# A transformer block on one Trainium2 core: keys, values and two retention heads join the projections that run while the conditioning weights load

## What is computed

```python
c_act = silu(c)
mod = c_act @ w_ada + b_ada                    # sh1, sc1, gt1, sh2, sc2, gt2
h = rms_norm(x, g_mix) * (1 + sc1) + sh1
rq, rk, rv, rg, aq, ak, av = split(h @ w_in + b_in)
ret = retention(rq, rk, rv, rg)                # 4 heads of 256, pairs rotated
att = window_sink_attention(aq, ak, av, sinks) # 16 query heads, 2 key heads of 64
x = x + gt1 * (concat(ret, att) @ w_out)
h = rms_norm(x, g_ffn) * (1 + sc2) + sh2
x = x + gt2 * conv_glu(h)                      # 2048 -> 2 x 5632 -> 2048
y = rms_norm(x, g_final) * (1 + f_scale) + f_shift
```

## Time and profile before

| | |
|---|---|
| median of 3 runs | 1285.28 us (1285.04 to 1286.55) |
| the profiled execution | 1290.68 us, its span 1289.0 us |
| PE busy | 1215.5 us, 94% of the span |
| DVE busy | 875.1 us, 68% |
| ACT busy | 590.5 us, 46% |
| moved by DMA | 343.03 MB |

### The profile page before, as it was taken

One profiled execution on the slowest core, in us unless ns is written; L12 is line 12 of the kernel. 1 busy time (PEld: TensorE's weight loads), 2 busy tenths in 40 slices (PEclk: granted clock), 3 DMA queues, 4 the chain that ended last, 5 costly groups with the idle time before them and its releaser, 6 DMA issues.

```text
span 1289.0 us, 22449 instructions
## 1 busy us (share of the span) xinstructions
PE 1215.5 (94%) x8031; PEld 1080.1 (84%) x8031; DVE 875.1 (68%) x1058; ACT 590.5 (46%) x849; POOL 174.7 (14%) x303
## 2 busy tenths in 40 slices
PE   5777799999999998999999999999999999999995
PEld 1545689897888786999999999999999987887884
DVE  1222478789698897566776767767655575778886
ACT  3221345426335345654454544545445454555442
POOL 6433111021121111000100100100000001010000
PEclk9778899999999998999999999999999999999998
DMA  9887998688699896468778787777655556887851
GB/s 358 323 309 283 350 331 287 236 301 318 239 349 348 308 336 232 163 218 287 263 276 275 265 287 264 277 273 266 209 176 182 185 189 245 286 290 253 328 214 65
DMA packets 117220, 343.03 MB, mean 266 GB/s; under 512 B 9806, under 2 KB 12336, under 8 KB 116528
## 3 DMA queue, kind: packets, MB, share of 16 engines
q1 hardware_dynamic: 79232, 206.19, 46.0%
q0 software_dynamic: 37504, 134.30, 28.6%
q10 hardware_dynamic: 432, 1.84, 0.4%
HBM read 340.20 MB, written 2.10 MB: 266 GB/s over the span
## 4 chain that ended last, share of the span: by engine, by line
PE 81%; DMA 7%; DVE 5%; issue 3%; ACT 2%; POOL 1%; POOLq 0%; ACTq 0%; DVEq 0%
PE ps L1167 26%; PE ps L1169 25%; PE ps L1168 25%; DMA arena<-in_w_ada 3%; DMA ada_raw<-in_w_ada 2%; DVE acc L767 2%; DMA raw<-in_w_in 1%; DVE wlo L757 1%; PE ps L1224 1%; PE ps L1213 1%; PE ps L1296 1%; DMA acc<-in_b_ada 1%; PE ps L1308 0%; DVE xb L1019 0%; DVE arena L1017 0%
## 5 line engine op out<-in xcount | busy, mean ns | idle before, releaser
L1167 PE MATMUL ps<-hhi,whi 128*128 128x256 f32 x1824 | 525.3, 288 | 27.0 <-DVE wlo L757 24.0
L1168 PE MATMUL ps<-hlo,whi 128*128 128x256 f32 x1824 | 520.3, 285 | 0.0
L1169 PE MATMUL ps<-hhi,wlo 128*128 128x256 f32 x1824 | 520.2, 285 | 0.0
L484 ACT ACTIVATE whi<-raw 128x1024 fp32r<-128x1024 f32 x248 | 262.7, 1059 | 346.7 <-PE ps L1169 345.2
L762 DVE TENSOR_TENSOR wlo<-raw,whi 128x1024 fp32r<-128x1024 f32 x248 | 303.3, 1223 | 134.2 <-ACT whi L484 132.3
L1167 PEld LDWEIGHTS ps<-hhi,whi 128*128 128x128 f32 x1824 | 355.5, 195 | 40.7 <-issue 35.8
L1168 PEld LDWEIGHTS ps<-hlo,whi 128*128 128x128 f32 x1824 | 355.6, 195 | 0.0
L1169 PEld LDWEIGHTS ps<-hhi,wlo 128*128 128x128 f32 x1824 | 355.2, 195 | 0.0
L767 DVE SCALAR_TENSOR_TENSOR acc<-ada_raw,c_act,acc 128x1024 f32<-128x1024 f32 (+1 forms) x192 | 245.9, 1281 | 10.4 <-DMA ada_raw<-in_w_ada 5.0
L1167 PE MATMUL ps<-whi,hhi 128*128 128x512 f32 x608 | 242.0, 398 | 3.2 <-DVE wlo L757 2.0
L1169 PE MATMUL ps<-whi,hlo 128*128 128x512 f32 x608 | 237.6, 391 | 0.0
(11 more groups left out here) (135 smaller groups left out, 615.7 us busy)
## 6 DMA issues: line engine op xcount, KB each, us to landing
raw<-in_w_up SPq DMA_DIRECT2D x176, 512.0 KB, 4.4
ada_raw<-in_w_ada POOLq DMA_DIRECT2D x160, 512.0 KB, 6.3
raw<-in_w_down SPq DMA_DIRECT2D x44, 1024.0 KB, 6.4
raw<-in_w_in SPq DMA_DIRECT2D x40, 1024.0 KB, 7.3
ada_raw<-in_w_final_ada POOLq DMA_DIRECT2D x64, 512.0 KB, 5.7
arena<-in_w_ada POOLq DMA_DIRECT2D x32, 512.0 KB, 9.1
raw<-in_w_out SPq DMA_DIRECT2D x16, 1024.0 KB, 7.5
xb<-in_x SPq DMA_DIRECT2D x2, 1024.0 KB, 6.1
```

What stands on the lines that cost most here:

```text
L484: nc.scalar.activation(whi[:, i % RING, :], raw_of(step0 + i), ACT.Copy).then_inc(hi_ready, 1)
L1167: nc.tensor.matmul(out_ap, lhs[0], rhs[0], start=start, stop=False, skip_group_check=skip)
L1168: nc.tensor.matmul(out_ap, lhs[0], rhs[1], start=False, stop=False, skip_group_check=skip)
L1169: return nc.tensor.matmul(out_ap, lhs[1], rhs[0], start=False, stop=True, skip_group_check=skip)
```

## The change

The front grows from 20 to 28 steps, seven for each job: four AQ steps, two steps that hold two k-tiles of retention heads 0 and 1 (`two_heads`), and one AK step. SP loads step 7*job + i when load i of the second turn of this job has landed. The retention queries that are left (heads 2 and 3) are eight steps (RQB). The program after the front is thus eight steps shorter: p counts to 55 before WO, and the step that had index p has p - 8. The PSUM banks are dealt out anew (`HEAD_BANK`; one bank for all conditioning sums).

```diff
-AQ_STEPS = [k if k < 12 else k + 3 for k in range(KT)]
-AK_STEPS = [12, 13, 14, 19]
+FRONT = 7
+AQ_STEPS = [FRONT * (k // 4) + (0, 1, 3, 4)[k % 4] for k in range(KT)]
+RQA_STEPS = [FRONT * (r // 2) + (2, 5)[r % 2] for r in range(KT // 2)]
+AK_STEPS = [FRONT * n + 6 for n in range(4)]
+STEP_RQB = 4 * FRONT
+HEAD_BANK = (5, 6, 7, 4)
 # SP
-            for i in range(6):
-                sp.wait_ge(ada_in[3], 16 * (i + 1))
-                load(i, w_in_k[:, 2 * i:2 * i + 2, COL_AQ:COL_AQ + GW])
+            for step in range(STEP_RQB):
+                job, i = divmod(step, FRONT)
+                sp.wait_ge(ada_in[i], 16 * (2 * job + 2))
...
 # DVE
+            for step in range(3):
+                lo(step)
             for job in range(4):
+                pe_rows(job)
                 mod_cols(job, 7, 8 * job)
-                h_lo(4 * job, 0)
...
+                for k in range(4 * job, 4 * job + 4):
+                    h_lo(k, 0)
+                for i in range(3, FRONT + 3 if job < 3 else FRONT):
+                    lo(FRONT * job + i)
+                    if job == 3 and i > 3:
+                        unit(i - 4)
 # PE
+            def two_heads(step, k0, heads, free=None):
+                pe.wait_ge(lo_ready, step + 1)
+                slot = step % RING
+                for h in heads:
+                    if free and h == heads[-1]:
+                        pe.wait_ge(*free)
+                    for kk in range(2):
+                        for e in range(2):
+                            first = kk * (GW // 2) + (h - heads[0]) * RD
+                            c = slice(first + e, first + RD, 2)
+                            last = passes(ps[:, HEAD_BANK[h], e * S:(e + 1) * S], (whi[:, slot, c], wlo[:, slot, c]),
+                                          (hhi[:, k0 + kk, :], hlo[:, k0 + kk, :]), k0 + kk + e == 0, True)
+                last.then_inc(step_done, 1)
...
             for job in range(4):
+                sum_columns(job, 7, 8 * job)
                 if job:
+                    keys_values(job - 1)
+                k = 4 * job
+                att_queries(k)
+                if job < 3:
+                    ada_pair(job + 1, 0)
+                att_queries(k + 1)
+                if job < 3:
+                    ada_pair(job + 1, 1)
+                two_heads(RQA_STEPS[2 * job], k, (0, 1))
+                if job < 3:
+                    ada_pair(job + 1, 2)
+                att_queries(k + 2)
+                if job < 3:
+                    ada_pair(job + 1, 3)
+                att_queries(k + 3)
+                if job < 3:
+                    for n in range(4, 8):
+                        ada_pair(job + 1, n)
+                two_heads(RQA_STEPS[2 * job + 1], k + 2, (0, 1))
...
 # PE: scores three to a step instead of two; second batch of heads two to a step (p 34 to 38)
-                elif 37 <= p < 46:
-                    att_head(1, p - 37)
+                elif 34 <= p < 39:
+                    for h in range(2 * (p - 34), min(2 * (p - 33), 9)):
+                        att_head(1, h)
```

More of the change, by code:

```diff
@@ L599, in mix_hi @@
                                      ACT.Copy).then_inc(hhi_ready, 1)
-            for p in range(STEP_WO0 - STEP_RQ):
-                hi(STEP_RQ + p)
+            for p in range(STEP_WO0 - STEP_RQB):
+                hi(STEP_RQB + p)
                 if p == 1:
@@ L780, in pe_rows @@
                 a = acc[:, acc_of(job), 0:512]
-                nc.vector.tensor_tensor(a, ps[:, 5 + job % 2, :], a, ALU.add).then_inc(ada_acc, 1)
+                nc.vector.tensor_tensor(a, ps[:, 7, :], a, ALU.add).then_inc(ada_acc, 1)
             def ada_turn(job, buf, turn, i):
@@ L833, in _ @@
                 nc.vector.tensor_copy(dst, ps[:, 4, col:col + count]).then_inc(cols_ready, 1)
-            pe_rows(0)
             dve.wait_ge(cols_ready, 4)
[L837 to L840, removed]
-                h_lo(4 * job, 0)
[L842 to L850, removed]
             def unit(n):
                 ada(4 + n // KT, n % KT)
[L855 to L858, removed]
+            for step in range(3):
+                lo(step)
+            for job in range(4):
+                pe_rows(job)
+                mod_cols(job, 7, 8 * job)
+                for k in range(4 * job, 4 * job + 4):
[4 more added lines that the diff above has]
+                        unit(i - 4)
             def values_out():
@@ L1008, in _ @@
                                                 ALU.subtract).then_inc(hlo_ready, 1)
-                for _ in range(units_at(STEP_WO0 - STEP_RQ + i)):
+                for _ in range(units_at(STEP_WO0 - STEP_RQB + i)):
                     unit(units)
@@ L1216, in ada_pair @@
             def ada_pair(job, n):
+                if job and n == 0:
+                    pe.wait_ge(mod_ready, job)
                 for j in range(2):
@@ L1223, in ada_pair @@
                         row = 32 * (2 * j + b)
-                        last = nc.tensor.matmul(ps[row:row + 32, 5 + job % 2, :], c_pad[:, k, :],
+                        last = nc.tensor.matmul(ps[row:row + 32, 7, :], c_pad[:, k, :],
                                                 ada_of_slot(slot)[:, b * 512:(b + 1) * 512],
@@ new lines, in att_queries @@
+            def att_queries(k):
+                pe.wait_ge(hlo_ready, k + 1)
+                pe.wait_ge(lo_ready, AQ_STEPS[k] + 1)
+                columns(AQ_STEPS[k] % RING, k, k == 0, lambda b: ps[:, b, :])
+            pe.wait_ge(cols_ready, 4)
+            for job in range(4):
+                sum_columns(job, 7, 8 * job)
+                if job:
+                    keys_values(job - 1)
[17 more added lines that the diff above has]
+                two_heads(RQA_STEPS[2 * job + 1], k + 2, (0, 1))
@@ L1290, in att_scores @@
+            keys_values(3)
             def att_scores(batch, i):
```

220 lines of the change are left out of this document (105 added, 115 removed).

## The result

The changed kernel takes 1295.61 us (median of 4 runs, 1295.34 to 1296.65), the kernel before beside it 1285.19 us (1285.04 to 1286.55). The ratio is 1.008, with a 95% interval of 1.0063 to 1.0098: slower by 10.4 us, where I had predicted 11.8 us less.

A forecast was written before the change was run, and what follows sets the result against it. PE, busy 94% of the span, was taken as the bound, with the front the soft place. Steps taken away behind the front -22.9, front +9.6, smaller terms +1.5 give -11.8 us from the median: 1273.5 us, range 1261 to 1285.

The forecast's parts named there:

- Landing: Front, a job's last conditioning loads: 8.5 us, between 7.5 and 9.3, so PE stands 2.6 us before pair 7.
- Start: Front, job 0: PE could start at 42.9, competing w_in loads delay it by 1.6 us, first step at 44.5.
- Turn: Front, between jobs: PE stands 3.3 us before the sum, 7.7 us with sum and AK step; clock loss 1.7 each.
- Behind the front: After the front: eight fewer steps take off 22.9 us, smaller terms add 1.5, bounds -1.2 and +4.
- The wait at p 14: Behind the front, ACT at p 11 to 13: 1.1 us of waiting for `lo`.
- The 1.6 us of waiting for DVE at p 34 to 40: Behind the front: DVE's 35 us of work minus overlaps against PE's 32, its lead thin, costing 1.6 us.
- its four fewer breaks save 0.2 each: Behind the front, head steps: a head step takes 4.35 us, and four fewer breaks save 0.2 us each.
- The scores: Behind the front: scores come three to a step, so two fewer breaks of 0.2 us each.
- Slower: Rival, front: each us of a job's last landing beyond 8.5 costs three; from 12.5 the change loses; 10%.
- DVE becomes the bound: Rival, behind the front: steps with units pay about 1 us more each, +8, total 1281 us; 8%.
- Covered: Rival, front: landings keep ahead of pair 7, clock stays up, front ends at 165.9, total 1260.6 us; 20%.
- the prediction's own signs of being wrong: A landing of 12 us, a front 20 us less or more, or `lo` waits over 5 us between p 30 and 50.

The follow-up runs named there:

- Run 3: The changed kernel with DVE's `pe_rows` ahead of the third remainder of the next job instead of behind it: 1276.97 us, ratio 0.9923 to the kernel before.
- run 1: The changed kernel with all seven w_in loads of a job released by the job's last conditioning load: 1313.99 us, ratio 1.0208 to the kernel before.
- Run 4: The changed kernel with ACT's `att_tile` of the second batch of heads one step later, behind the probability copies: 1292.22 us, ratio 1.0044 to the kernel before.
- run 2: The changed kernel with PE's conditioning pairs two by two, ahead of the loads that they release: 1283.26 us, ratio 0.9965 to the kernel before.
- run 6: The changed kernel with pairs two by two and `pe_rows` ahead of the third remainder: 1266.52 us, ratio 0.9845 to the kernel before.
- run 10: The changed kernel with pairs two by two, `pe_rows` earlier, head copies a step later, no unit at p 13 to 16: 1262.15 us, ratio 0.9801 to the kernel before.

## Why the prediction was wrong

The reading of what is soft and what is full was right: the steps behind the front came off in full, and the front paid. It was the front's price that failed, 26.3 us instead of 9.6. Two terms of the sum carry most of that. *Landing* was put at 8.5 us and took 10.5 to 11.7. The way from pair 7 to the next job's first step, which holds the turn and its clock, was put at 13.3 us and took 14.2 to 16.5. The terms, as measured in the first trace:

| term of the prediction | predicted | measured | too little by |
|---|---|---|---|
| first step starts | 44.5 | 45.8 | 1.3 |
| four steps, each with a pair: job 0, then jobs 1 and 2 | 17.6, then 15.6 | 19.1, then 16.1 | 2.4 |
| pair 3's end to pair 7 | 8.5 | 10.5, 11.3, 11.7 | 8.0 |
| pair 7 to the next job's first AQ step | 13.3 | 14.3, 14.2, 16.5 | 5.1 |
| last job behind its turn, seven steps | 20.1 | 20.1 | 0 |

Together 16.8 us, which leads from the 178.8 of the prediction to 195.6. By the medians the forecast is off by more, 22.2 us. The other 5.4 us are its base: 169.2 for the front of before came from a trace 5.4 us above the median, but the difference was taken from the median. The second trace of before, at the median of its set, has its front done at 166.0. So some 3 us of that excess lay in the very stretch that I compared with.

**Start.** I wrote that "the step's `lo` is now made ahead of the sum, so PE could start at 42.9 instead of 44.96". It is made ahead of the sum, and just that is the fault: three `lo` stand before `pe_rows`. The third needs even the fourth w_in load, because the loads of steps 2 and 3 count up one semaphore, and `hi` of either waits for both (`raw_value` counts 32). That load was issued at 25.84 and landed at 38.85. The chain shows how it goes on: `hi` at 38.87, `pe_rows` at 41.10, sum at 41.93. I had asked whether the conditioning loads would be late by the competition, not whether a w_in load would be. They were not: the last one of job 0 landed at 35.2, and before at 36.0. That 44.5 came near 45.8 is luck, since the delay that it counts is another one. Run 3 gives 2.6 us back here.

**Landing.** I took 8.5, "between 7.5 and 9.3". My own count of three and a half loads at even shares gave 9.3, and the measured landings are 9.06, 9.91 and 10.30; the competition was the cause, as run 1 shows. What I had left out is the time from pair 3's end to the issue of the last load, 1.4 us each time (66.18 is 1.36 behind the pair's end), since the two loads that the pair releases are issued one after the other, 0.7 us apart. The two queues while the first of these landings went on (66 to 75 us):

```profile
q0 software_dynamic: 596, 1.96, 56.0%
q1 hardware_dynamic: 571, 1.60, 45.8%
```

Near-equal packets, and 55% of the bytes for the conditioning loads (q0). The Trainium skill says in "DMA: Bandwidth & Descriptors", section "Queues, rings and completion order", that an engine takes turns between its queues by the packet. The packet counts agree with that; what doesn't hold here is what I had worked out from it, that w_in would take over half of the bytes and a landing would be 12.6 us. It rested on a wrong size: I gave the conditioning loads pieces of 2 KB, but in the trace 478 of q0's 596 packets have 4096 bytes and the rest 128 or 4, while w_in's larger ones are 256 of 4096 and 268 of 2048 bytes. The 0.30 MB in 129 packets of the earlier trace rows came from 56 such small ones. No last load of jobs 1 to 3 took 12.6 us, except where pairs two by two had put more into the queue ahead.

**Turn.** The wait before the sum was foreseen, place, cause and size: 3.3 predicted, 3.06 measured. Its clock was not. I put 1.7 us on each turn, which is 3.4 us of half clock, from one row. The trace has two waits per turn, 3.2 to 3.9 us before the pairs and 3.06 before the sum. At the first turn the clock is at half for 6.8 us behind the sum; at the second behind both waits, 116.8 to 120.2 and 127.0 to 130.4; at the third behind both for 6.8 us each. That makes 27.2 us at the lower level where I had counted 10.2. Run 3 measures what the wait before the sum was worth: 19.2 us in the front, of which 3 x 3.06 + 2.6 is standing. The rest, some 7 us, agrees with the clock, whose lower level lasts 13.6 us less in these jobs; one trace a side can't give it closer. I had found this wait in the order of DVE's program and treated it as given. That is no error of the sum, but the missed chance: I priced it and did not ask what the 12 us of idle DVE beside it meant.

**Behind the front** the sum was right, -21.4 against -21.1, its parts less so. The wait at p 14 came (1.41, predicted 1.1), with half clock behind it. The 1.6 us of waiting for DVE at p 34 to 40 did not; PE's waits there are for ACT. For "its four fewer breaks save 0.2 each" of the heads the trace has the opposite: the batch costs 16.7 us beyond its plain steps instead of 12.0, since the packing moved the copies behind `att_tile` and `hi`. Run 4, without that stall, is at 11.8: the packing itself saves nothing that can be told. The scores saved more than I gave them: a step with three costs 1.05 us more than a plain one, as one with two does, so two fewer are 2.1. What made up the difference is that each trace of before holds a loss of some 4 us that after has not: in the first the wait and half clock of the earlier trace rows, in the second that wait and a fall of the clock at the sums of p 46. So that the total agrees to 0.3 us is partly luck.

**The rivals.** "Slower" had the right sign, but not the mechanism: pair 3's end to pair 7 stayed under the 12.5 us from which it was to decide. The loss needed both the landing and the turn, which I had kept apart, as if only one of them could go wrong. That either one of the two edits in the front takes the loss away shows it (runs 2 and 3: 0.9965 and 0.9923). "DVE becomes the bound" was wrong as to place: DVE bounds nothing by its amount of work (68%), but by its order it does, at the start, at each turn and at p 14. "Covered" is what run 6 comes to: front done at 167.7, against 165.9 in that rival. And of the prediction's own signs of being wrong none came in jobs 1 to 3 or behind them: no last landing of 12 us, no front off by 20 us (16.8), no `lo` wait of 5 us. They were set so wide that the forecast could fail inside them.

## What to carry to other kernels

Where an engine with an order of its own makes a result that another waits for, look at what stands ahead of it and what that needs. Here one remainder, needed three steps later, stood before the one addition that PE waited for; putting them the other way round was worth 19 us.

A wait in the bound engine is priced with the work behind it that runs at half clock, and each wait by itself: here 3.06 us of standing cost 4.9 to 6.5 (10.2, 8.6 and 9.9 us a turn against 3.7). And where a forecast is counted from the median, its rows should come from an execution near the median.

A landing's time is no cost as such. When the queue was filled earlier (run 2) each landing took longer and the kernel got faster; what counts is issue plus landing against the moment of need. Before a transfer is moved away, ask what it is ahead of in every other engine's order.

## What the runs showed of the hardware

The clock can fall without PE having stood. At p 39 PE makes 32 matmuls with a single column each (`sum_columns`), with no idle time before or behind. In run 4, the sum, and the windows around it:

```profile
342.84 4.05 PE L1209 MATMUL ps<-ones,acc 128*128 128x1 f32 x32
```

```profile
342.80:346.00 3.20, 3.20 (x30) 3.16 (x29) 2.10 (x2) 1.06 (x1) 0.53 (x1) 0.98 1.03 408
346.00:352.00 6.00, 6.00 (x17) 4.86 (x17) 6.00 (x10) 0.00 (x0) 0.53 (x1) 0.50 1.00 384
```

From 346 on the granted clock is 0.50 of 2.4 GHz, that is 1.2 GHz, though PE is busy without a gap. In the changed kernel the same sum takes 3.62 us and the clock stays at 1.00:

```profile
354.00:358.00 4.00, 4.00 (x36) 3.91 (x35) 0.25 (x3) 1.06 (x1) 0.00 (x0) 1.00 1.01 407
358.00:362.00 4.00, 4.00 (x19) 3.28 (x18) 4.00 (x6) 1.06 (x1) 0.00 (x0) 1.00 0.59 241
```

The second trace of before shows the fall there, its first does not. Over all thirteen traces the stretch from the end of the step ahead of these sums to the end of the next takes 6.35 us in three (the first of before and both of the changed kernel) and 7.9 to 9.5 us in ten. So the same instructions cost up to 3 us more or less from one trace to the next. Falls in the front do the same: runs 6 and 10 have the same front, with no half clock and 13.6 us of it in jobs 1 to 3, and end it 6.0 us apart. This is likely why runs of one kernel here lie 3 to 11 us apart, but with one trace or two of each it is not shown. A difference of this size between two single traces is not a finding. I have not tested what decides it.
